# Order of a head norm, a scaled product and a conditioning product in a two-block transformer kernel on one core

## What is computed

```python
# first block, recurrent half of the mixer: 4 heads of 128
rec = hgrn2_chunkwise(gq, gf, gi, lbs[l])
rec = rmsnorm(rec, hgrn_norm_g[l]) * jax.nn.silu(gg...)
h = h + jnp.concatenate([fox_out, rec], axis=-1) @ w_out[l]

# second block: each of two layers is conditioned on the vector c
cond = jax.nn.silu(c)
mod = cond @ ada_w[layer] + ada_b[layer]              # 1024 x 6144 per layer
sh1, sc1, g1, sh2, sc2, g2 = jnp.split(mod, 6, axis=-1)
...
x = x + g2[:, None, :] * swiglu(modulate(rms_norm(x), sh2, sc2), ffn_w1[layer], ffn_w3[layer], ffn_w2[layer])
# swiglu: (silu(h @ w1) * (h @ w3)) @ w2, hidden width 2816
```

## Time and profile before

| | us |
|---|---|
| median of 3 runs | 2089.91 |
| lowest, highest run | 2089.61, 2094.29 |
| profiled execution, its own time | 2092.28 |
| its span, first to last instruction | 2090.5 |

### The profile page before, as it was taken

One profiled execution on the slowest core, in us unless ns is written; L12 is line 12 of the kernel. 1 busy time (PEld: TensorE's weight loads), 2 busy tenths in 40 slices (PEclk: granted clock), 3 DMA queues, 4 the chain that ended last, 5 costly groups with the idle time before them and its releaser, 6 DMA issues.

```text
span 2090.5 us, 26023 instructions
## 1 busy us (share of the span) xinstructions
PE 2032.4 (97%) x10142; PEld 1688.6 (81%) x10142; DVE 1203.1 (58%) x1955; ACT 749.7 (36%) x1023; POOL 890.1 (43%) x488
## 2 busy tenths in 40 slices
PE   7999899999999999998998999999999899999998
PEld 6878787988888888876787888888888788888887
DVE  5454656546889895668577777616665763111112
ACT  5344434333513222546552222224353343222221
POOL 3322424754344444345343444443553334444442
PEclk9999999999999999999999999999999999999999
DMA  4322202516577862240259778423341023223321
GB/s 142 108 84 79 76 1 94 163 67 151 132 196 186 198 163 93 70 135 21 56 126 203 184 181 197 121 86 96 102 143 51 31 81 95 95 93 101 101 91 71
DMA packets 227631, 233.41 MB, mean 112 GB/s; under 512 B 6699, under 2 KB 222580, under 8 KB 227388
## 3 DMA queue, kind: packets, MB, share of 16 engines
q1 hardware_dynamic: 227008, 231.71, 39.5%
q10 hardware_dynamic: 508, 0.12, 0.0%
HBM read 229.56 MB, written 2.24 MB: 111 GB/s over the span
## 4 chain that ended last, share of the span: by engine, by line
PE 86%; DVE 6%; issue 3%; ACT 2%; DMA 2%; POOL 1%; ACTq 0%; SPq 0%; DVEq 0%; POOLq 0%
PE ps L2349 21%; PE ps L2351 20%; PE ps L2350 20%; PE ps L2400 7%; PE ps L2405 3%; PE ps L3189 1%; PE ps L3175 1%; POOL wL L625 1%; PE ps L2862 1%; DMA raw<-in_w_xkv_dram 1%; PE ps L2793 1%; DVE adacc L1884 1%; ACT wH L787 1%; DVE ssum L1411 1%; PE ps L2643 1%
## 5 line engine op out<-in xcount | busy, mean ns | idle before, releaser
L625 POOL TENSOR_TENSOR wL<-raw,wH 128x1024 fp32r<-128x1024 f32 (+2 forms) x322 | 773.8, 2425 | 1023.6 <-ACT wH L787 962.4
L787 ACT ACTIVATE wH<-raw 128x2048 fp32r<-128x2048 f32 (+2 forms) x161 | 302.5, 1879 | 459.7 <-PE ps L2351 318.6
L2349 PE MATMUL ps<-uH,wH 128*128 128x512 f32 x1088 | 427.5, 393 | 10.0 <-issue 6.1
L2351 PE MATMUL ps<-uH,wL 128*128 128x512 f32 x1088 | 425.2, 391 | 0.0
L2350 PE MATMUL ps<-uL,wH 128*128 128x512 f32 x1088 | 425.0, 391 | 0.0
L1884 DVE SCALAR_TENSOR_TENSOR adacc<-adaw,adab,adacc 128x256 f32<-128x256 f32 x372 | 294.3, 791 | 13.1
L2349 PE MATMUL ps<-hnH,wH 128*128 128x512 f32 x728 | 287.4, 395 | 0.0
L2351 PE MATMUL ps<-hnH,wL 128*128 128x512 f32 x728 | 283.7, 390 | 0.0
L2350 PE MATMUL ps<-hnL,wH 128*128 128x512 f32 x728 | 283.2, 389 | 0.0
L2349 PEld LDWEIGHTS ps<-uH,wH 128*128 128x128 f32 x1088 | 205.4, 189 | 55.7 <-issue 9.8
L2351 PEld LDWEIGHTS ps<-uH,wL 128*128 128x128 f32 x1088 | 205.1, 189 | 43.3
(11 more groups left out here) (461 smaller groups left out, 3054.0 us busy)
## 6 DMA issues: line engine op xcount, KB each, us to landing
raw<-in_ffn_w_dram SPq DMA_DIRECT2D x60, 1024.0 KB, 5.4
adaw<-in_ada_w_dram SPq DMA_DIRECT2D x192, 256.0 KB, 7.2
raw<-in_w_dram SPq DMA_DIRECT2D x32, 1024.0 KB, 5.7
raw<-in_w_in_dram SPq DMA_DIRECT2D x14, 1024.0 KB, 5.5
raw<-in_od_w_in_dram SPq DMA_DIRECT2D x12, 1024.0 KB, 5.3
raw<-in_w_xkv_dram SPq DMA_DIRECT2D x8, 1024.0 KB, 5.6
raw<-in_ffn_w_dram SPq DMA_DIRECT2D x8, 768.0 KB, 4.3
raw<-in_ev_w_in_dram SPq DMA_DIRECT2D x5, 1024.0 KB, 5.4
```

What stands on the lines that cost most here:

```text
L625: nc.gpsimd.tensor_tensor(wL[n % 2][:, k0:k1, 0:c], raw[n % 2][:, k0:k1, 0:c], wH[n % 2][:, k0:k1, 0:c].bitcast(F32), ALU.subtract).then_i ...
L787: nc.scalar.activation(wH[n % 2][:, 0:kc, 0:c], raw[n % 2][:, 0:kc, 0:c], ACT.Copy).then_inc(w_hi, 1)
L2349: nc.tensor.matmul(out_ap, wh, xh, start=first, stop=False)
L2351: return nc.tensor.matmul(out_ap, wl, xh, start=False, stop=last)
```

## The change

Three edits, with the same instructions on every engine.

1. The four heads' sums on TensorE, one piece of 16 matmuls between the first four chunks of unit 0 and of unit 1, are made head by head between those chunks.
2. In the scaling of the heads on DVE, each head's scaling is put ahead of the low part of the head before.
3. In the first pass of the first gated layer DVE takes pair p ahead of tiles 2p and 2p + 1, for p from 1 to 3 (pair 0 was so already). On TensorE the sums of tiles 0 to 3 move from the middle of unit 4 to that of unit 6, and those of tiles 4 to 7 from unit 8, fifth chunk, to the middle of unit 9.

```diff
             for h in range(HG_H):
                 dve.wait_ge(h_bc, h + 1)
                 if h >= 2:
                     dve.wait_ge(op_lo, Q0["mix"] + 4 + h - 1)
                 nc.vector.tensor_tensor(T[h % 2][:], ps[(5, 6, 7, 4)[h]][:], gg[:, h, :], ALU.mult).then_inc(op_t, 1)
-                low_op(Q0["mix"] + 4 + h, uL[:, 4 + h, :], T[h % 2][:], uH[:, 4 + h, :])
+                for x in (h - 1,) if 0 < h < HG_H - 1 else (h - 1, h) if h else ():
+                    low_op(Q0["mix"] + 4 + x, uL[:, 4 + x, :], T[x % 2][:], uH[:, 4 + x, :])
...
                     for p in range(4):
-                        if i == 0 and p == 0:
-                            pair(0, 0)
-                            cond(0, 0)
-                            cond(0, 1)
-                            continue
+                        if i == 0:
+                            pair(p, 0)
                         cond(i, 2 * p)
                         cond(i, 2 * p + 1)
-                        pair(p, i)
+                        if i:
+                            pair(p, i)
...
-            output_chunks(0, range(0, KC // 2))
-            for h in range(HG_H):
+            output_chunks(0, (0, 1))
+
+            def head_sums(h):
                 pe.wait_ge(h_sq, h + 1)
                 ...
                 ins.then_inc(h_sum, 1)
+
+            head_sums(0)
+            output_chunks(0, (2,))
+            head_sums(1)
+            output_chunks(0, (3,))
+            head_sums(2)
             unit_ready(AT["out"][0] + 1)
-            output_chunks(1, range(0, KC // 2))
+            output_chunks(1, (0,))
+            head_sums(3)
+            output_chunks(1, (1, 2, 3))
...
-                        if layer == 0 and i == 0 and u < 5:
-                            inside = {4: {"between": lambda: conditioning_sums(1, 0, 3)}}.get(u, {})
+                        if layer == 0 and i == 0:
+                            inside = {6: {"between": lambda: conditioning_sums(1, 0, 3)},
+                                      9: {"between": lambda: conditioning_sums(1, 0, 7)}}.get(u, {})
```

## The result

| | before | after |
|---|---|---|
| median of the runs, us | 2089.91 (5 runs, 2089.34 to 2094.29) | 2099.28 (5 runs, 2097.19 to 2102.04) |
| profiled execution, its own time and span, us | 2092.28, 2090.5 | 2099.28, 2097.5 |
| TensorE's mean granted clock | 0.987 | 0.988 |

The ratio after to before is 1.0036, with a 95% interval of 1.0021 to 1.0050; the medians lie 9.4 us apart, the profiled executions 7.0. The prediction was 2090.3 us in a range of 2085.5 to 2095.8: wrong, and its slower rival, priced at 2098, is close to what happened.

The account below looks back on a forecast made before the run. TensorE, busy 97% of the span, was taken as the bound. The terms -1.65 - 1.8 + 2.3 + 0.9 + 0.2 gave -0.05 us, so 2089.9 from the median; stated as 2090.3 us, range 2085.5 to 2095.8.

Parts of the forecast that it names:

- Head sums, -1.65 us: Output stage: spreading the sums between chunks keeps the clock from falling behind them, saving 1.65 us (bounds 0 and 1.65).
- Scaled chunks, -1.8: Output stage: scaling the next head ahead of each subtraction cuts three steps from 1.99 to 1.39 us, saving 1.8 us.
- Nothing lost behind them: After the output stage: both gains, 3.45 us, go on to the next stages.
- The mechanism of the stalls: Gated layer, first pass: tile m+4's loads wait for tile m's multiply-adds, and unit m+4's 1 MB weight load queues behind them.
- c2 is done at 1127.7, just ahead of GpSimd's split of unit 5 at 1127.92: Gated layer, first pass: tile 2's eight multiply-adds on VectorE finish before that split begins, with a margin of 0.2 us.
- Unit 6: no stall: Gated layer, first pass: unit 6's weights come in time for TensorE, with 1 us to spare.
- Unit 8, 2.3 us: Gated layer, first pass: TensorE stalls 1.4 to 3.3 us before unit 8, taken as 2.3.
- Unit 10, 0.9: Gated layer, first pass: TensorE stalls 0 to 1.8 us before unit 10, taken as 0.9.
- Clock, 0.2: Gated layer: short stalls cost no clock; one of 3 us and more may, for 1.65 us; 0.2 us put in.
- Rival 2: Gated layer: late conditioning tiles starve the weight queue, units 6, 8 and 10 stall, clock falls twice; +8 us, 2098, chance 0.11.
- Rival 1: Gated layer: tile 4's multiply-adds slip past GpSimd's split, which waits instead; -1.85 us, 2088.1, chance 0.2.
- Rivals 3 and 4: Unit 4's load gets the queue alone, 2082 us, chance 0.04; clock falls behind head sums anyway, +1.65 us, chance 0.1.

Follow-up runs that it names:

- e5: The kernel before with only the head sums spread between output chunks (edit 1); one run, 2084.58 us beside 2087.02 of before.
- e6: The kernel before with only each head's scaling put ahead of the previous head's low part (edit 2); one run, 2093.82 us beside 2087.02 of before.
- e7: The kernel before with only tiles 2 and 3 put one pair later on VectorE; one run, no time given, unit 6 2.62 us late.
- e8: The kernel before with only tiles 4 to 7 put one pair later on VectorE; one run, no time given, units 8 and 10 2.4 and 2.9 us late.
- e3: The changed kernel with SyncE issuing each tile behind its own unit's weights, one unit later; 2081.32 us, ratio 0.9949 to before.
- e4: The two output-stage edits, old gated-layer order, with SyncE issuing each tile behind its own unit's weights, one unit later; 2078.61 us, ratio 0.9938 to before.
- e14: The changed kernel with four unused 256 KB DMAs issued on SyncE behind unit 5's weights; one run, no time given, those weights landed after 14.77 us.
- e13: The changed kernel with only GpSimd's split of unit 5 made to wait for tile 2's multiply-adds; one run, 2094.80 us.
- e10: The changed kernel with GpSimd's splits of units 5, 7 and 9 made to wait for tiles 2, 4 and 6; 2088.33 us, ratio 0.9984 to before.
- e2: The kernel before with the gated-layer edit alone (edit 3); 2100.86 us, ratio 1.0048 to before.
- e1: The kernel before with the two output-stage edits alone (edits 1 and 2); 2088.41 us, ratio 0.9985 to before.
- e11: e3 with the sums of tiles 4 to 7 in the middle of unit 10 instead of unit 9; 2080.72 us, ratio 0.9944 to before.
- e9: The changed kernel with unit 5's weights issued only once ScalarE has made unit 4's high part; one run, 2095.45 us.
- e12: e4 measured once more, unchanged; 2080.08 us, ratio 0.9935 to before.

## Why the prediction was wrong, step by step

- **Head sums, -1.65 us: right.** -1.62 by e5, with the granted clock at 1.00 where it was 0.50.
- **Scaled chunks, -1.8: right.** -1.90 by e6; both together -3.48 against -3.45. They are additive.
- **Nothing lost behind them: right.** The shift is still there at the gated layer (split of unit 3 at 1091.18 instead of 1095.57, 4.39 us; 0.49 of it stood before the output stage, and 0.4 more I didn't trace).
- **The mechanism of the stalls: right.** The weights of unit m + 4 stand behind the loads of tile m + 4, which wait for tile m (e7, e8; e3 and e4 take the path away). Unit 4's wait stayed, 6.26 us.
- **"c2 is done at 1127.7, just ahead of GpSimd's split of unit 5 at 1127.92": the step that failed.** I moved VectorE's work and left GpSimd's split where the earlier trace rows has it. But its landing (1125.90, 16.0 us after its issue, where ScalarE starts in the earlier trace rows) had been made late by the loads of tile 6, which the change itself takes out from behind it. They landed 13.5 us after the issue. Counted from before's issue at 1109.88, the split comes at about 1125.4 instead of 1127.92, a margin of 0.2 us against a movement of 2.5. e14 puts such loads back and gets half of it. By e13 this step is worth 4.1 us of the stretch.
- **"Unit 6: no stall": failed with it.** 1.51 us. Where tile 2 is freed (e10, e13) there is none.
- **Unit 8, 2.3 us: right in e13 (2.35), too small after (3.93).** In e13 too tile 4 is caught by both halves (multiply-adds of 2.50 us at 1145.03 and 1147.56), where 2.3 stood for one, so the agreement is in part luck. The upper bound had been 3.3, with both halves of the split on tile 4. That is what happens; on top of it comes that tile 4 begins later, behind pair 2, whose subtractions lie beside the late split of unit 6 and take 4.06 us (1141.58) instead of 1.48 (1146.20 before).
- **Unit 10, 0.9: a second failed step.** The sum had "4.2 for c6", that is, tile 6 caught by nothing; it put the whole split of unit 9 on tile 7, without working out when unit 9's weights land. Tile 6 is caught by both halves, as tile 4 is: 3.07 us after and 2.69 in e13. With all three tiles freed (e10) both stalls vanish.
- **Clock, 0.2: mis-sized.** Each of the two stalls brought 3.4 us at half clock, 3.4 us lost in all, the largest single miss of the sum. I had reasoned from 2.39 us idle without a fall; in e13 2.35 us had a fall behind them, and in e2 3.36 us ahead of unit 8 had none. The length of an idle time did not tell by itself whether the clock fell.
- **Sum:** -3.48 where -3.45 stood, and +12.9 where +3.4 stood. The 9.5 us of difference are 1.5 for unit 6, 1.6 for unit 8, 2.2 for unit 10, 3.2 for the clock, 0.2 for unit 4 and the 0.8 not traced. Of these, e13 gives back 4.1 with tile 2 freed; the greater part is unit 10's step and the clock's. From arriving 4.4 us sooner and losing 12.9 the changed kernel is 8.5 us behind, and of that 1.5 us came back later: before has 6.8 us at half clock from 1559.5, which the changed kernel has not, and the changed kernel has 3.4 more at 1674.8. I read this as scatter between executions: of the sixteen traces five have half clock from a point between 1551 and 1567 (before, e1, e2, e6 and e11), among them e1 and e2, which share no edit.

The rows before and after, in that order:

```profile
1559.50:1566.30 6.80, 6.80 (x20) 4.15 (x19) 2.56 (x7) 2.37 (x6) 6.72 (x11) 0.50 0.51 163
```
```profile
1565.00:1571.80 6.80, 6.17 (x25) 3.58 (x26) 4.13 (x10) 5.41 (x9) 6.45 (x6) 1.00 0.79 206
1674.80:1678.20 3.40, 3.40 (x16) 3.40 (x17) 2.39 (x7) 0.00 (x0) 0.00 (x0) 0.51 0.00 0
```

- **The rivals.** Rival 2 named the mechanism, the place and nearly the time (2098 against 2099.28; its +8 us against +9.4 by the medians and +7.0 by the profiled executions), and I gave it 0.11, because an earlier split, the queue's longer time and both falls of the clock had to come together. They did not have to: in e13, where tile 2 is free, units 8 and 10 still stall, each with a fall of the clock. That its price came so near is in part luck, for unit 6 stalled 1.51 us where it had 3, and unit 10 3.07 where it had 1.8. Rival 1 did not occur: at each of these meetings VectorE lost 2 us (2.50 instead of 0.48), and tile 4 was caught by both halves. GpSimd lost a little too: its split of unit 5 in e10, beside multiply-adds, takes 5.22 us and that of unit 6, beside none, 4.75, a difference of the length of one multiply-add. That agrees with what the Trainium skill says (SBUF — State Buffer, SBUF: two separate sides): whoever starts first has the shared port pair, and the other blocks. In the changed kernel the first half of unit 5's split starts at 1121.05, beside a multiply-add that runs until 1121.31, and takes 2.52 us where a half beside none takes 2.39 in e10; the next multiply-add, started beside it, takes 2.50. I read this as GpSimd waiting for the short instruction that runs, then VectorE for the long one. Rivals 3 and 4 didn't occur: unit 4's wait was 6.26 us, and the clock behind the sums 1.00.

## What to carry to other kernels

When an edit moves work between engines that share a queue, move every row that hangs on the queue before comparing two of them: a margin of 0.2 us between one row that was moved and one that was left where the old trace had it is no margin. Look for the load that stands behind another load's wait; here issuing each tile one unit later in the queue's program (e4, 9.8 us under e1 by the medians) was worth more than all three edits, and took away a stall of 6 us that had looked like a given. Where a chance is made small because several mishaps must coincide, ask of each whether it really needs the others: here the stalls of units 8 and 10 came with or without that of unit 6. And where one meeting of two engines is worked out for one tile, work it out for the next ones too.

## What I had not expected of the hardware

- The same 1 MB load of unit 5 took 5.3 us from issue to landing when nearly alone (e9), 13.5 us behind the loads of unit 4 and tile 5 (after), 14.8 with four loads issued behind it too (e14), 16.0 in the kernel before. What was issued behind this load delayed it.
- TensorE at half clock turns up for 3.4, 6.8 or 13.7 us at places that no edit touched (1557 in e6 for 13.7 us, 1559.5 in before for 6.8, not at all there in after). At 13.7 us these alone move a single run by 7 us, which is as much as the change is worth.
- Like idle times did not have like effects on the clock: 2.35 us idle with half clock behind it in e13, 2.38 us at 1651.77 in e12 with the clock at 1.00, and 3.36 us ahead of unit 8 in e2 with the clock at 1.00 from 1168.0 to 1174.8.

```profile
1651.77 0.35 PE L3185 MATMUL ps<-vx,wt 128*128 128x129 f32 x1 [2.38 <-DVE hs L2269]
```
```profile
1651.77:1655.17 3.40, 3.40 (x28) 3.11 (x28) 3.40 (x8) 0.62 (x3) 1.27 (x1) 1.00 0.02 5
```
